# Three products of 256 columns into one sum in the feed-forward layers of a three-layer network

## The reference, cut to what matters

```python
def swiglu_ffn(h, w_in, w_out):                      # layers 0 and 1, hidden width 2816
    gate, up = jnp.split(h @ w_in, 2, axis=-1)
    return (jax.nn.silu(gate) * up) @ w_out
...
    h = rmsnorm(x, g_pre_mlp)                        # last layer, hidden width 4096
    ff = jnp.einsum('blf,fd->bld', jnp.square(jax.nn.relu(jnp.einsum('bld,df->blf', h, w_ff1))), w_ff2)
    return x + rmsnorm(ff, g_post_mlp)
```

## Time and profile before

| | us |
|---|---|
| median of 3 runs | 1346.68 |
| lowest and highest | 1345.7, 1347.03 |
| span of the profiled execution | 1342.6 |
| TensorE busy in it | 1271.3 (95%) |
| VectorE busy | 865.9 (64%) |
| ScalarE busy | 507.1 (38%) |

### The profile page before, as it was taken

How to read it: one execution, slowest core, us unless ns; L and a number is a source line. 1 busy time by engine, 2 the same in 40 slices (tenths; PEclk the granted TensorE clock), 3 DMA queues, 4 the chain that set the end, 5 groups by cost and what they waited for, 6 DMA issues and landing times. The chain is left out here.

```text
span 1342.6 us, 19019 instructions
## 1 busy us (share of the span) xinstructions
PE 1271.3 (95%) x7198; PEld 985.6 (73%) x7198; DVE 865.9 (64%) x1505; ACT 507.1 (38%) x857; POOL 124.1 (9%) x165
## 2 busy tenths in 40 slices
PE   3999979989999998999999999899999999899997
PEld 1787645554888887874688888687778785688886
DVE  0547886444777775886777776499952432777776
ACT  2664266324544444014644443302123312544443
POOL 0061021000000002000000000255520000000000
PEclk9999989999999998999999999999999999899999
DMA  9322376984655542421555555033324323455551
GB/s 390 128 82 95 134 299 267 386 318 172 218 187 187 189 155 81 148 92 54 190 210 189 188 189 202 33 126 141 141 95 142 112 100 118 161 188 187 188 187 60
DMA packets 24949, 225.78 MB, mean 168 GB/s; under 512 B 2737, under 2 KB 2865, under 8 KB 4658
## 3 DMA queue, kind: packets, MB, share of 16 engines
q1 hardware_dynamic: 23328, 220.31, 45.0%
q10 hardware_dynamic: 1554, 4.56, 1.0%
HBM read 223.81 MB, written 1.05 MB: 167 GB/s over the span
## 5 line engine op out<-in xcount | busy, mean ns | idle before, releaser
L894 PE MATMUL psum<-aT_r,arena_r 128*128 128x512 f32 x920 | 327.7, 398 | 1.5 <-DVE arena_r L2221 1.3
L2221 DVE TENSOR_TENSOR arena_r<-ring,arena_r 128x1024 fp32r<-128x1024 f32 x188 | 220.2, 1220 | 106.5 <-ACT arena_r L1622 106.5
L809 PE MATMUL psum<-aT,ring 128*128 128x256 f32 (+1 forms) x1136 | 265.3, 391 | 0.0
L895 PE MATMUL psum<-aT_r,arena_r 128*128 128x256 f32 x920 | 258.1, 281 | 0.0
L809 PEld LDWEIGHTS psum<-aT,ring 128*128 128x128 f32 x1136 | 214.1, 191 | 45.9 <-issue 18.8
L1622 ACT ACTIVATE arena_r<-ring 128x1024 fp32r<-128x1024 f32 x188 | 186.8, 1051 | 149.8 <-PE psum L929 133.6
L929 PE MATMUL psum<-arena_r 128*128 128x512 f32 x876 | 213.4, 392 | 0.0
L894 PEld LDWEIGHTS psum<-aT_r,arena_r 128*128 128x128 f32 x920 | 172.9, 188 | 44.2 <-issue 2.2
L929 PEld LDWEIGHTS psum<-arena_r 128*128 128x128 f32 x876 | 159.5, 188 | 34.8
L895 PEld LDWEIGHTS psum<-aT_r,arena_r 128*128 128x128 f32 x920 | 173.8, 189 | 2.6
L1634 ACT ACTIVATE nrm<-nrm 128x256 f32<-128x256 f32 x76 | 31.8, 418 | 164.6 <-DVE nrm L2239 161.4
(11 more groups left out here) (499 smaller groups left out, 1620.7 us busy)
## 6 DMA issues: line engine op xcount, KB each, us to landing
ring<-in_w_ffn SPq DMA_DIRECT2D x44, 1536.0 KB, 6.6
ring<-in_w_mod SPq DMA_DIRECT2D x32, 1536.0 KB, 8.9
ring<-in_w_ff SPq DMA_DIRECT2D x32, 1024.0 KB, 4.9
ring<-in_w_in_g SPq DMA_DIRECT2D x8, 1536.0 KB, 6.4
ring<-in_w_conf_i SPq DMA_DIRECT2D x8, 1024.0 KB, 4.9
ring<-in_w_hyb_f SPq DMA_DIRECT2D x4, 1536.0 KB, 6.5
ring<-in_w_in_a SPq DMA_DIRECT2D x4, 1536.0 KB, 6.4
ring<-in_w_in_b SPq DMA_DIRECT2D x4, 1536.0 KB, 6.8
```

The lines of the kernel that those rows point to most:

```text
L809: last = mm(bank(use)[:, out_at:out_at + rhs(k).shape[1]], weights[:, k * P:(k + 1) * P], rhs(k), start=(k == 0), stop=(k == KT - 1))
L894: mm(bank(use).rearrange("p (a t) -> p a t", a=2), hi, x_both[:, :, k, :], start=(k == 0), stop=False)
L895: last = mm(bank(use)[:, T:2 * T], lo, x_hi[:, k, :], start=False, stop=(k == KT - 1))
L2221: tt(lo, slot(c)[:, at], hi.bitcast(F32), ALU.subtract).then_inc(split_ready, 1)
```

## The change

For each k-tile of each part, `block_in` issues three products of 256 columns, hi x hi, hi x lo, lo x hi, all into the left half of the bank, where they accumulate into one sum. The sums of halves on VectorE, the buffers `g_sum` and `u_sum`, the view `x_both` and two semaphores are gone. ScalarE's function reads the gate's bank itself and frees it; VectorE's multiplication reads the up part's bank in PSUM. `first_block`, `block_out`, the splits and the DMAs are untouched.

```diff
-        x_both = view(aT_r, 0, 2, KT, T)
...
-                            mm(bank(use).rearrange("p (a t) -> p a t", a=2), hi, x_both[:, :, k, :], start=(k == 0), stop=False)
-                            last = mm(bank(use)[:, T:2 * T], lo, x_hi[:, k, :], start=False, stop=(k == KT - 1))
+                            for wp, xp in ((hi, x_hi), (hi, x_lo), (lo, x_hi)):
+                                last = mm(bank(use)[:, 0:T], wp, xp[:, k, :], start=(k == 0 and wp is hi and xp is x_hi),
+                                          stop=(k == KT - 1 and wp is lo))
...
                     if j + 1 < n and (j or name == "ffn1"):
                         split(name, j + 1, range(parts - 1), i)
+                    act.wait_ge(bank_full[uses[j][0]], uses[j][1] + 1 + AGAIN * i)
+                    if j >= 2:
+
+                        act.wait_ge(h_step, 2 * (base + j - 2) + 1 + 2 * SLOTS * i)
+                    opened = fn(sg[:, j % 2, :], bank(uses[j])[:, 0:T], func)
                     if parts == 3:
-                        act.wait_ge(bank_free[uses[j][0]], uses[j][1] + 1 + AGAIN * i)
+                        freed(opened, uses[j])
                     else:
-                        act.wait_ge(in_sum, j + 1 + SLOTS * i)
-                    fn(sg[:, j % 2, :], g_sum[:, j % 2, :], func).then_inc(act_on, 1)
+                        opened.then_inc(act_on, 1)
...
-                    gate = USE[name][j]
-                    dve.wait_ge(bank_full[gate[0]], gate[1] + 1 + AGAIN * i)
-                    if j >= 2:
-                        dve.wait_ge(act_on, base + j - 1 + SLOTS * i)
-                    whole = isinstance(i, int) and j == 0
-                    if whole:
-                        summed = v.tensor_copy(g_sum[:, 0, :], bank(gate)[:, 0:T])
+                    gate, up = USE[name][j], uses[j]
+                    if parts == 3:
+                        dve.wait_ge(bank_free[gate[0]], gate[1] + 1 + AGAIN * i)
+                        dve.wait_ge(bank_full[up[0]], up[1] + 1 + AGAIN * i)
                     else:
-                        summed = v.reduce_sum(g_sum[:, j % 2, :], bank(gate).rearrange("p (a t) -> p t a", a=2), axis=AXX)
...
-                            v.reduce_sum(u_sum, bank(uses[j]).rearrange("p (a t) -> p t a", a=2), axis=AXX).then_inc(up_sum, 1)
...
-                    tt(h_tmp, sg[:, j % 2, :], u_sum if parts == 3 else sg[:, j % 2, :], ALU.mult).then_inc(h_step, 1)
+                    other = bank(up)[:, 0:T] if parts == 3 else sg[:, j % 2, :]
+                    tt(h_tmp, sg[:, j % 2, :], other, ALU.mult).then_inc(h_step, 1)
```

More of the change, by code:

```diff
@@ L423, in build @@
         sg, h_tmp = view(nrm_t, 0, 2, T), nrm_t[:, 2 * T:3 * T]
-        g_sum, u_sum = view(nrm_t, 3 * T, 2, T), nrm_t[:, 5 * T:6 * T]
         small = sb("small", 480)
@@ L584, in build @@
         h_step = sem("h_step")
-        in_sum, up_sum = sem("in_sum"), sem("up_sum")
         act_on = sem("act_on")
@@ L1625, in ffn @@
                 uses, parts = USE[name], FFNS[name][0]
+                base = {"ffn0": 0, "ffn1": NF, "ff": 2 * NF}[name]
                 def one(j, i=0):
@@ L2230, in one @@
                         split(name, j + 1, range(parts - 1), i)
-                    gate = USE[name][j]
-                    dve.wait_ge(bank_full[gate[0]], gate[1] + 1 + AGAIN * i)
-                    if j >= 2:
-                        dve.wait_ge(act_on, base + j - 1 + SLOTS * i)
-                    whole = isinstance(i, int) and j == 0
-                    if whole:
-                        summed = v.tensor_copy(g_sum[:, 0, :], bank(gate)[:, 0:T])
-                    else:
-                        summed = v.reduce_sum(g_sum[:, j % 2, :], bank(gate).rearrange("p (a t) -> p t a", a=2), axis=AXX)
[L2240 to L2245, removed]
-                            v.reduce_sum(u_sum, bank(uses[j]).rearrange("p (a t) -> p t a", a=2), axis=AXX).then_inc(up_sum, 1)
-                    else:
-                        summed.then_inc(in_sum, 1)
-                    dve.wait_ge(act_on, base + j + 1 + SLOTS * i)
+                    gate, up = USE[name][j], uses[j]
+                    if parts == 3:
+                        dve.wait_ge(bank_free[gate[0]], gate[1] + 1 + AGAIN * i)
+                        dve.wait_ge(bank_full[up[0]], up[1] + 1 + AGAIN * i)
+                    else:
+                        dve.wait_ge(act_on, j + 1 + SLOTS * i)
                     if j:
@@ L2253, in one @@
                     step = 2 * (base + j) + 2 * SLOTS * i
-                    if parts == 3:
-                        dve.wait_ge(up_sum, base + j + 1 + SLOTS * i)
-                    tt(h_tmp, sg[:, j % 2, :], u_sum if parts == 3 else sg[:, j % 2, :], ALU.mult).then_inc(h_step, 1)
+                    other = bank(up)[:, 0:T] if parts == 3 else sg[:, j % 2, :]
+                    tt(h_tmp, sg[:, j % 2, :], other, ALU.mult).then_inc(h_step, 1)
                     b = 2 if j == n - 1 else j % 2
```

## The result

The changed kernel takes 1351.34 us (median of 6 runs, 1349.23 to 1355.18), the kernel before 1346.19 us beside it (6 runs, 1342.9 to 1347.87). The ratio is 1.004, with a 95% interval of 1.0025 to 1.0056: 0.4% **slower**, where 0.3% faster was forecast. The profiled execution has a span of 1347.6 us against 1342.6. The changed kernel's six runs fall in two groups, three from 1349.23 to 1349.41 and three from 1353.26 to 1355.18; the profiled one is of the first, and no trace shows what the others spend.

What follows compares the result with a forecast made beforehand. TensorE's own pace was taken to bound the feed-forward layers. -1.8 (products) - 2.0 (sums) - 0.2 (tail) = -4.0 us, so 1346.7 became 1342.7 us, 0.3% faster, with a range of 1335.5 to 1352.

Steps and rivals of the forecast that it cites:

- What bounds the kernel: In the three feed-forward layers TensorE, busy 529.1 of 531.0 us, sets the time; VectorE and ScalarE have slack.
- Step 1: TensorE's input products before the change: a pair of 512 and 256 columns takes 352 to 354 ns.
- Step 2: TensorE's input products after: three of 256 columns take 351 ns a tile, -2 ns, so -1.8 us over 920 tiles.
- The bound on the slow side: TensorE's input products: a fixed price of 16 ns per product would add 16 ns a tile, +15 us.
- quiet-pace rival: TensorE's input products: 113 ns per 256 columns, 339 a tile, -12.9 us and the tail, 1333.6 us; chance 0.12.
- The bound on the fast side: TensorE's input products: at 111 ns each, three take 333 ns, -20 ns a tile, -18 us.
- Step 3: VectorE's sums of halves go, 78.8 us: direct gain nothing, less traffic beside TensorE -2.0 us (between 0 and 3.2).
- Step 4: Bank freeing and waits: nothing is late in the loop; at the last layer's end TensorE's 0.2 us wait goes.
- the tail: End of the last layer: without the reduction, TensorE's 0.2 us wait before its last products goes.
- The rival of a price per product: TensorE's input products: fixed price or exposed third load, +16 ns a tile, +15.2 us, 1359.7 us; chance 0.15.
- The two rules of the page: TensorE: loads overlap only in another row group, else near 100 us more; 2.5 ns fixed per product, 2.3 us.

Runs made afterwards that it cites:

- e5_six_128: The changed kernel with every product of 256 columns cut in two of 128, except the very first of a part; 1625.16 us in one run.
- e2_engines_only: The changed kernel with the former products of 512 and 256 columns put back, sums of halves still gone; 1346.28 us, 0.9998 of the kernel before.
- e9_grouped_no_sums: The kernel before without sums of halves, each part's eight 512-column products issued first, then its eight of 256; 1339.14 us, ratio 0.9948.
- the grouped order: The kernel before with each part's eight products of 512 columns first, then its eight of 256, sums kept; 1339.95 us, ratio 0.9954.
- e6_320_192: The kernel before, high and low activations side by side, its 512-column product cut into 320 and 192 columns; 1368.05 us, ratio 1.0158.

## Why the prediction was wrong

**What bounds the kernel**: right. TensorE's pace decided, and all of the change in time lies there.

**Step 1**, 352 to 354 ns a pair: right as a sum. The split into 232 to 236 and 117 to 118 was read rightly from the start times, but it isn't the price of the two sizes. Among its like, a product of 512 columns takes 227 ns and one of 256 takes 120; in the alternation the first is 5 to 9 ns longer and the second 2 to 3 shorter.

**Step 2 is the step that failed**: "Three of them are 351 ns against 352 to 354". The three are 360. The argument was that line 895's own 117 ns held everything that a product with a load needs. It was a distance between two starts, out of a sequence in which the neighbour's distance is longer; carried to a sequence without that neighbour it no longer held. The sum over a whole period, 352 to 354, was a sound number, but of that sequence alone. The bound on the slow side (33 ns over the columns of a pair, 16 for each product) had the right mechanism, and was a little high: 13 for each, three of them 40, 7 ns over a pair that held 33. The rows had shown half of it: 226 ns for 512 columns in a row of equal products, which the prediction itself set at "13 over 213". The other half, 120 for 256, stands in no row of before; side by side the two say 13 ns a product at either size. The prediction halved the 226 for its quiet-pace rival, and so halved the price with it. The bound on the fast side had no ground either: the 111 ns "with its own load" are of plain float32 products, whose 128 columns take 107 by themselves; that e5_six_128 found 111 for the float32r product as well is luck. And the prediction named its weakest place rightly: "3 ns more on each 256-column product turns -4.0 into +4.3 us". It was 3 ns more.

**Step 3**, -2.0 us for the sums of halves: wrong in its indirect part. The direct gain is nothing, as said; e2_engines_only and e9_grouped_no_sums show that the indirect one is nothing too. The 4% between a pair at 0.34 and one at 0.354 is the place of the pair and not a quiet neighbourhood: each block's first pair has it, 440.33 to 440.67 as well, and in e2_engines_only, without the sums, it is 426.12 to 426.45. ScalarE's read of PSUM, put at 473 ns, takes 385; this moved nothing.

**Step 4**: right. The timeline of the changed kernel at the end of the last layer:

```profile
1330.27 3.10 PE L892 MATMUL psum<-aT_r,arena_r 128*128 128x256 f32 x24 [0.77 <-DVE arena_r L2224]
...
1333.21 2.00 PE L927 MATMUL psum<-arena_r 128*128 128x512 f32 x8
...
1334.62 0.42 DVE L2253 TENSOR_TENSOR z_r<-nrm,z_r 128x256 fp32r<-128x256 f32 x1
```

The low part is ready at 1335.04, and twelve output products from 1333.21 (the row shows the first eight) last to 1335.96, so nothing waits for it. What remains there, 0.77 us for VectorE's split, was there before (0.83 at the same place; the earlier trace rows have two such waits). ScalarE's wait for VectorE (161.4 us) is gone from its list.

**The sum.** Forecast -1.8 - 2.0 - 0.2 = -4.0 us. Measured by the same terms: +5.6 for the pace (the output products' 0.03 us a block in the last layer included), 0 for the sums, -0.2 for the tail, +5.0 in the span. The rival of a price per product was the right mechanism, with a chance of 0.15 and 1359.7 us. Its +16 ns a tile came to +7: 13 for the third product, less the 6 that the pairs took over their two prices; without the 2.0 us for the sums that is 1346.7 + 6.4 - 0.2 = 1352.9 by its own sum, against 1351.3 measured. The sign of the forecast was wrong; that the time lay inside the range is owed to the part of this rival that the range took in.

**The two rules of the page.** The float32r products here show a fixed price of 13 ns besides the columns. The page "TensorE: Matmul & The Clock Gate" of the Trainium skill has such a price in its section on the back-to-back issue gap, of 2.5 ns for products one behind the other. That was the right kind of rule, since it speaks against the change, but it would make +2.3 us. And 2760 loads, each beside a product, at 120 ns contradict again what the same page of the Trainium skill says of what overlaps: that a load runs beside a product only in another row group.

**Open**: why the alternating pairs take 6 ns over the two prices in most blocks and nothing in a few, and two equal neighbours nothing. The layout of the columns and the sums were tried and are not it; plain float32 products or a wait just ahead of a block go with the better pace in three cases of four, and no run tried them. In the grouped order something of it is left where 512 columns come back behind 256 in a block: eight products take 2.00 us there in place of 1.98. Open too is the 0.03 us a block that the output products of the last layer give back when pairs do not alternate.

## What to carry to other kernels

The float32r products here cost their columns and a fixed price, so for a given number of columns the fewest and widest products win, and saving work on an engine with slack does not pay for one more product on the engine that bounds. Read the price of a size from a row of equal products; a distance between two starts in a mixed sequence belongs to the sequence. And where two sizes alternate, try them in groups of two or more: here that was worth 0.5%, with the same products.

## What the runs showed of the hardware

- The price of a float32r product besides its columns is near 13 ns at 256 and 512 columns (120 and 227 ns), at the 2.4 GHz level; the 0.14 to 0.15 us at 320 columns agree with it. The 107 ns between the two sizes are one cycle a column.
- In plain float32 it is near 3 ns a record. Two rows of the mixers in the changed kernel:

```profile
559.63 4.70 PE L806 MATMUL psum<-aT,ring 128*128 128x256 f32 x21
```

```profile
646.85 5.31 PE L837 MATMUL psum<-ring,arena 128*128 128x512 f32 x12
...
652.87 1.88 PE L837 MATMUL psum<-ring,arena 128*128 128x512 f32 x4
```

  (4.70 - 0.38)/20 = 216 ns for a record of 256 columns and (5.31 - 1.88)/8 = 429 for one of 512. The difference, 213 ns for 256 columns, is two cycles a column; 3 ns are left. A plain product shows as two such records (`first_block` has 80 products and 160 records).
- A row of float32r products of 128 columns, each with its load, goes at 111 ns, where columns and price would be 67. By these numbers the floor ends at (111 - 13) x 2.4 = 235 columns, an estimate. A single shorter distance is possible: 0.09 us behind the 192 columns of e6_320_192, made up by the next.
- Products of 512 and 256 columns in turn take 353 ns a pair in most blocks and 347 in a few; in twos or eights, 346 to 347.
